# Seven half-size products for three of four second feed-forward products, and strips' low parts on GpSimd in the first attention

## The reference, cut to what matters

```python
h = h + jnp.concatenate([att, ssd], axis=-1) @ w_out[i]
hn = rmsnorm(h, norm_mlp_w[i])
h = h + jnp.square(jax.nn.relu(hn @ w_ff1[i])) @ w_ff2[i]
```

## Time and profile before

| | us |
|---|---|
| median of 3 runs | 1649.72 |
| lowest and highest | 1649.25, 1651.26 |
| the profiled execution | 1650.62 |
| its span in the trace | 1648.9 |

### The profile page before, as it was taken

The page is one execution under the profiler, slowest core; times in us unless marked ns, Lnnn a source line. Parts: engine busy times, 40 slices in busy tenths (PEclk is TensorE's granted clock), DMA queues, the critical chain, the costliest instruction groups (busy, mean ns, idle before and its releaser), DMA issues.

```text
span 1648.9 us, 19185 instructions
## 1 busy us (share of the span) xinstructions
PE 1619.0 (98%) x7688; PEld 1334.3 (81%) x7688; DVE 964.1 (58%) x1388; ACT 670.9 (41%) x1011; POOL 171.4 (10%) x244
## 2 busy tenths in 40 slices
PE   7999999999999999999999999999999999999998
PEld 6878777788888888887788877888888888888787
DVE  6745688674343434656844568544567727735757
ACT  5534375543222313414672146442334414414544
POOL 0001135100000000003710146000000000000000
PEclk9999999999999999999999999999999999999999
DMA  5224231122222222231122221322232222222321
GB/s 186 77 79 146 84 128 52 58 96 102 103 85 95 102 102 101 107 130 72 52 77 103 77 77 51 129 101 81 99 115 103 90 90 102 102 103 84 121 102 52
DMA packets 27992, 157.30 MB, mean 95 GB/s; under 512 B 3776, under 2 KB 6272, under 8 KB 10752
## 3 DMA queue, kind: packets, MB, share of 16 engines
q1 hardware_dynamic: 23184, 145.52, 24.5%
q10 hardware_dynamic: 4720, 10.56, 1.8%
HBM read 151.84 MB, written 4.23 MB: 95 GB/s over the span
## 4 chain that ended last, share of the span: by engine, by line
PE 88%; DVE 7%; issue 2%; ACT 2%; POOL 1%; DMA 0%; POOLq 0%; SPq 0%; DVEq 0%; ACTq 0%
PE bank L586 24%; PE bank L588 24%; PE bank L587 24%; PE bank L594 2%; PE bank L596 2%; PE bank L595 2%; PE bank L789 1%; PE bank L774 1%; PE bank L885 1%; DVE w_lo L1625 1%; DVE w_lo L1618 1%; PE bank L758 1%; PE bank L759 1%; PE bank L1061 0%; PE bank L1063 0%
## 5 line engine op out<-in xcount | busy, mean ns | idle before, releaser
L586 PE MATMUL bank<-a_hi,w_hi 128*128 128x512 f32 x1184 | 467.8, 395 | 9.0 <-DVE w_lo L1820 8.4
L588 PE MATMUL bank<-a_hi,w_lo 128*128 128x512 f32 x1184 | 462.2, 390 | 0.0
L587 PE MATMUL bank<-a_lo,w_hi 128*128 128x512 f32 x1184 | 461.8, 390 | 0.0
L1106 ACT ACTIVATE w_hi<-w_raw 128x2048 fp32r<-128x2048 f32 x120 | 228.9, 1908 | 280.1 <-DMA w_raw<-in_strips 276.7
L1618 DVE TENSOR_TENSOR w_lo<-w_raw,w_hi 128x2048 fp32r<-128x2048 f32 x118 | 270.1, 2290 | 16.4 <-ACT w_hi L1106 16.2
L586 PEld LDWEIGHTS bank<-a_hi,w_hi 128*128 128x128 f32 x1184 | 223.4, 189 | 54.1 <-DVE w_lo L1820 8.4
L588 PEld LDWEIGHTS bank<-a_hi,w_lo 128*128 128x128 f32 x1184 | 222.8, 188 | 46.8
L587 PEld LDWEIGHTS bank<-a_lo,w_hi 128*128 128x128 f32 x1184 | 223.2, 189 | 44.6 <-issue 0.2
L586 PE MATMUL bank<-b_hi,w_hi 128*128 128x512 f32 x560 | 218.2, 390 | 1.1 <-DVE w_lo L1618 0.6
L587 PE MATMUL bank<-b_lo,w_hi 128*128 128x512 f32 x560 | 217.9, 389 | 0.0
L588 PE MATMUL bank<-b_hi,w_lo 128*128 128x512 f32 x560 | 217.8, 389 | 0.0
(11 more groups left out here) (329 smaller groups left out, 2111.7 us busy)
## 6 DMA issues: line engine op xcount, KB each, us to landing
w_raw<-in_strips SPq DMA_DIRECT2D x132, 1024.0 KB, 4.8
...
```

Source lines behind the costliest of these rows:

```text
L586: mm(ps[:, :], w_hi[slot][:, k, cols], hi[:, k, :], start=(k == 0), stop=False)
L587: mm(ps[:, :], w_hi[slot][:, k, cols], lo[:, k, :], start=False, stop=False)
L588: return mm(ps[:, :], w_lo[slot][:, k, cols], hi[:, k, :], start=False, stop=(k == kt - 1))
L1106: run(w_hi[j], w_raw[j], ACT.Copy).then_inc(hi_split, 1)
```

## The change

**Seven products.** For groups 0 to 2 (`SEVEN`), the product of the hidden values (512 tokens x 1024) with 1024 x 1024 of `w_ff2` is no longer made as eight units. Hidden values T are cut into halves by tokens and by features, the weights A into halves by rows and by columns, and Strassen's seven products of sums of such halves give the four quarters of the result. A product is 256 tokens x 512 by 512 x 512: two token tiles, four feature tiles, three matmuls each, so 24 matmuls of 128x512, now with the hidden values as the stationary side. `T_PARTS` and `A_PARTS` say which halves go into product i, and with what sign; five of the seven have a sum on each side.

ACT squares `relu` once, into `hid` (no split). POOL makes the sums: `a_sums` adds two loaded quarters of the weights (`a_part`, 128x2048) into the strip's `w_raw`, `t_sums` adds two halves of `hid` (128x1024) into `t_raw`. ACT makes the high parts (`a_high`, `t_high`), DVE the low parts (`a_low` 128x2048, `t_low` 128x1024). Products 2 and 6 stay in banks 4 to 7 over the three groups; the banks of the other five are added to `added` tiles by DVE (`add_product`). SP loads the quarters instead of `w_ff2` strips (four of 1 MB a group, as many as before), and the first strip of the next `ff1` goes to a tile `spare`.

**The last group** keeps its two phases as they were. During `ff1_3`, DVE makes the quarters of the result out of `added` and the kept banks in eleven operations one behind the other (`c_step`; five of 128x1024, six of 128x512), PE transposes them back to features in eight times four transposes between its matmuls (`turn_c`), and DVE adds these to `x`.

**The first attention.** The low parts of four strips (the last three of `wo_ssd` and the first of `wo_att`), 16 quarters of 128x512, go from DVE to POOL (`low_quarter`), one in every second slot, behind POOL's `normalize` and copies of that slot. A fifth strip stays with DVE.

```diff
+SEVEN = [f"ff2_{g}" for g in range(FF_GROUPS - 1)]
+T_PARTS = [((0, 0), None, 0), ((1, 0), (0, 0), -1), ((0, 0), (1, 1), 1), ((1, 0), (1, 1), 1), ((0, 0), (0, 1), 1), ((1, 1), None, 0),
+           ((0, 1), (1, 1), -1)]
+A_PARTS = [((0, 1), (1, 1), -1), ((0, 0), (0, 1), 1), ((0, 0), (1, 1), 1), ((0, 0), None, 0), ((1, 1), None, 0), ((1, 0), (0, 0), -1),
+           ((1, 0), (1, 1), 1)]
+T_SUMS = [i for i in range(7) if T_PARTS[i][2]]
+A_SUMS = [i for i in range(7) if A_PARTS[i][2]]
+KEPT = {2: 4, 6: 6}
+ADDED = [i for i in range(7) if i not in KEPT]
+A_PLACE = {(0, 1): 0, (1, 0): 0, (1, 1): 1, (0, 0): 2}
+PHASES += [(f"{w}{g}", 7 if f"{w}{g}" in SEVEN else 4) for g in range(FF_GROUPS) for w in ("ff1_", "ff2_")]
...
                                  d["strips"][0][:, h * (SW // 4):(h + 1) * (SW // 4)]).then_inc(x_loaded[h], 16)
                 sp_eng.dma_start(x[:, two, :], d["x_t"][:, two, :]).then_inc(x_loaded[h], 16)
+            def load_part(part, g):
...
+                    if g == 0:
+                        sp_eng.wait_ge(unit_done, 2 * FIRST["ff1_0"])
...
+                    sp_eng.wait_ge(a_sum, A_SUM0 + len(A_SUMS) * g + 2)
+                    load_part((1, 0), g)
...
+                    s = FIRST["wo_ssd"] + 1 + q // 4
+                    j, part = s % W_SLOTS, slice(2 * (q % 4), 2 * (q % 4) + 2)
+                    if q % 4 == 0:
+                        pool.wait_ge(hi_split, s)
+                        pool.wait_ge(strip_split, s)
+                    ins = pool.tensor_tensor(w_lo[j][:, part], w_raw[j][:, part], w_hi[j][:, part].bitcast(F32), ALU.subtract)
+                    if q % 4 == 3:
+                        ins.then_inc(strip_split, 1)
...
+                    if not causal and n < TILES and n % 2 == 0:
+                        low_quarter(n // 2)
...
+            def a_sums(g, i):
+                one, two, sign = A_PARTS[i]
+                s = FIRST[SEVEN[g]] + i
+                for part in (one, two):
+                    pool.wait_ge(part_loaded[A_PLACE[part]], part_count(part, g))
+                pool.wait_ge(unit_done, 2 * (s - W_SLOTS) + 2)
+                pool.tensor_tensor(w_raw[s % W_SLOTS].rearrange("p k n -> p (k n)"), a_part[A_PLACE[one]], a_part[A_PLACE[two]],
+                                   ALU.add if sign > 0 else ALU.subtract).then_inc(a_sum, 1)
+            def t_sums(g, i):
+                one, two, sign = T_PARTS[i]
+                q = 7 * g + i
+                pool.wait_ge(hid_done, HID0 + KT * g + (W4 if one[1] + two[1] == 0 else KT))
+                pool.wait_ge(unit_done, product_done(q - 3))
+                pool.tensor_tensor(t_raw[q % 3], hid_half(one), hid_half(two), ALU.add if sign > 0 else ALU.subtract).then_inc(t_sum, 1)
+            for g in range(len(SEVEN)):
+                a_sums(g, 0)
+                t_sums(g, 1)
+                a_sums(g, 1)
+                a_sums(g, 2)
+                t_sums(g, 2)
+                t_sums(g, 3)
+                t_sums(g, 4)
+                a_sums(g, 5)
+                a_sums(g, 6)
+                t_sums(g, 6)
...
-            def ff_group(g, norm):
-                stream("ff1_0", feature_k, A, ready=wait_tiles(NORMS["mlp"]["lo"]), strips=8 * g, fills=16 * g,
-                       after=(lambda j: direct_sums("mlp") if j == 0 else None) if norm else None)
-                stream("ff2_0", feature_k, B, ready=lambda k: pe.wait_ge(inner_lo, KT * g + k + 1), strips=8 * g, fills=16 * g)
...
+                for i in range(7):
+                    s, q = FIRST[phase] + i, 7 * g + i
+                    slot, hi, lo = s % W_SLOTS, t_hi[q % 3], t_lo[q % 3]
+                    pe.wait_ge(strip_split, s + 1)
+                    pe.wait_ge(t_low_done, T_LOW0 + q + 1)
+                    for t in range(2):
+                        tok = slice(t * P, (t + 1) * P)
+                        if i in KEPT:
+                            ps, first, end = bank[KEPT[i] + t], g == 0, g == len(SEVEN) - 1
+                        else:
+                            f = 2 * ADDED.index(i) + t
+                            ps, first, end = bank[f % 4], True, True
+                            bank_free(phase, f)
+                        for k in range(W4):
+                            mm(ps[:, :], hi[:, k, tok], w_hi4[slot][:, k, :], start=(first and k == 0), stop=False)
+                            mm(ps[:, :], hi[:, k, tok], w_lo4[slot][:, k, :], start=False, stop=False)
+                            last = mm(ps[:, :], lo[:, k, tok], w_hi4[slot][:, k, :], start=False, stop=(end and k == W4 - 1))
+                        last.then_inc(unit_done, 1)
...
+                    pe.wait_ge(c_step, C_STEP0 + 11)
+                if m >= 4:
+                    pe.wait_ge(c_added, C_ADDED0 + m - 3)
+                for t in range(TT):
+                    src = c_part[t // 2, m // 4][:, t % 2, m % 4 * P:(m % 4 + 1) * P]
+                    last = tr(bank[4 + m % 4][:, t * P:(t + 1) * P], src, ident)
+                last.then_inc(c_turned, 1)
+            C_TURNS = {(5, 1): 0, (5, 3): 1, (5, 5): 2, (5, 7): 3, (6, 3): 4, (6, 4): 5, (6, 5): 6, (6, 6): 7}
...
+            for g in range(FF_GROUPS):
+                stream(f"ff1_{g}", feature_k, A, ready=wait_tiles(NORMS["mlp"]["lo"]),
+                       after=(lambda j: direct_sums("mlp") if j == 0 else None) if g == 0 else None,
+                       within=within_last if g == FF_GROUPS - 1 else None)
+                if g < len(SEVEN):
+                    seven(g)
+            stream(f"ff2_{FF_GROUPS - 1}", feature_k, B, ready=lambda k: pe.wait_ge(inner_lo, k + 1))
...
+                for step, i in ((a_high, 2), (t_high, 2), (a_high, 3), (t_high, 3), (a_high, 4), (t_high, 4), (t_high, 5), (a_high, 5),
+                                (a_high, 6), (t_high, 6)):
+                    step(g, i)
+                s = FIRST[f"ff1_{g + 1}"]
+                act.wait_ge(spare_loaded, SPARE0 + 16 * (g + 1))
+                act.wait_ge(unit_done, 2 * (s - W_SLOTS) + 2)
+                run(w_hi[s % W_SLOTS], spare, ACT.Copy).then_inc(hi_split, 1)
+                hi(s + 1)
...
-                        lo_part(FIRST[phase] + 1, n - 2)
                     if lead is None and not wide and n < 4:
                         lo_part(FIRST[phase] + 1, n)
                     for part in range(4):
                         for i in slot_splits(n - part, call, wide, 1) if 0 <= n - part < SLOTS else ():
-                            lo_part(FIRST[phase] + i, part)
+                            if causal:
+                                lo_part(FIRST[phase] + i, part)
+                            elif i == 5:
+                                dve.wait_ge(strip_split, FIRST[phase] + i)
+                                lo_part(FIRST[phase] + i, part)
...
+            def a_low(g, i):
+                s = FIRST[SEVEN[g]] + i
+                j = s % W_SLOTS
+                dve.wait_ge(hi_split, s)
+                src = w_raw[j].rearrange("p k n -> p (k n)") if A_PARTS[i][2] else a_part[A_PLACE[A_PARTS[i][0]]]
+                v.tensor_tensor(w_lo[j].rearrange("p k n -> p (k n)"), src, w_hi[j].bitcast(F32).rearrange("p k n -> p (k n)"),
+                                ALU.subtract).then_inc(strip_split, 1)
...
+                q = 7 * g + i
+                dve.wait_ge(t_high_done, T_HIGH0 + q + 1)
+                src = t_raw[q % 3] if T_PARTS[i][2] else hid_half(T_PARTS[i][0])
+                v.tensor_tensor(t_lo[q % 3], src, t_hi[q % 3].bitcast(F32), ALU.subtract).then_inc(t_low_done, 1)
...
+            def add_product(g, i):
+                for t in range(2):
+                    f = 2 * ADDED.index(i) + t
+                    dst, src = added[i][:, t, :], bank[f % 4][:, :]
+                    dve.wait_ge(unit_done, 2 * (FIRST[SEVEN[g]] + i) + t + 1)
+                    if g:
+                        dve.wait_ge(dve_evac, EVAC0[SEVEN[g - 1]] + f + 1)
+                    ins = v.tensor_tensor(dst, dst, src, ALU.add) if g else v.tensor_copy(dst, src)
+                    ins.then_inc(dve_evac, 1)
...
-                    dve.wait_ge(inner_hi, n + 1)
+                    relu_evac(g, j)
+                    if j == 0 and g:
+                        lo(FIRST[f"ff1_{g}"] + 2)
+                    if j == 3:
+                        lo(FIRST[f"ff1_{g}"] + 3)
+                    if j == 5:
+                        t_low(g, 0)
+                        a_low(g, 0)
+                    if j == 6:
+                        t_low(g, 1)
+                        a_low(g, 1)
+                for step, i in ((add_product, 0), (a_low, 2), (t_low, 2), (a_low, 3), (t_low, 3), (add_product, 1), (a_low, 4), (t_low, 4),
+                                (t_low, 5), (add_product, 3), (a_low, 5), (a_low, 6), (t_low, 6), (add_product, 4)):
+                    step(g, i)
+                s = FIRST[f"ff1_{g + 1}"]
+                dve.wait_ge(hi_split, s)
```

(33 more changed lines are left out.)

192 lines of the change are left out of this document (156 added, 36 removed).

## The result

The changed kernel takes 1688.64 us (median of 4 runs, 1686.43 to 1690.74), the kernel before 1650.05 (4 runs, 1649.25 to 1651.26): ratio 1.0233, 95% interval 1.0215 to 1.0251. It is slower by 38.6 us; I had forecast 1680, between 1655 and 1700. The spans of the two profiled executions lie 36.9 us apart (1685.8 and 1648.9), and all that follows is counted in them.

The account below looks back on a forecast made before the run. PE's matmuls were taken to bound the kernel. -16.3 (fewer matmuls) + 3.5 (transposes) + 2.5 (last group) + 40.5 (POOL/DVE exclusion) = +30.2 us on 1650.6: 1680.8, median 1680, range 1655 to 1700.

Parts of the forecast that it names:

- -16.3 us for fewer matmuls: Groups 0 to 2: seven products replace eight units, 24 matmuls less a group, 5.44 us three times, -16.3 us.
- Transposes +3.5: Last group: eight times four transposes on PE between its matmuls, 0.44 us each time, +3.5 us.
- first wait +2.5: `ff1_3`: PE waits in unit 5 for DVE's eleventh operation on the result's quarters, +2.5 us, at its cheapest 0.
- POOL's price: POOL's two-input sums: 4.5 us for 2048 columns, 2.35 for 1024, 1.27 for a quarter of 512.
- Mutual exclusion: POOL's sums and DVE's low parts never overlap: whichever starts first blocks the other fully; stalls of +40.5 us in three groups.
- The rival of 1639: Long POOL operations exclude DVE for less than their length, so no product is late: 1639 us, chance 0.15.
- 13.5 us of waits a group: Groups 0 to 2: PE's waits before late products, from group 1 scheduled by hand; +40.5 us for three groups.
- The clock: First feed-forward part: the granted clock was read as 1.00; the forecast has no term for a change of it.
- exclusion at the expected prices: POOL and DVE exclusive, a 2048-column sum taking 3.95 to 5.1 us: forecast 1680, own range 1667 to 1688, chance 0.65.
- The first attention, 0: First attention: moving 16 quarters from DVE to POOL taken as 0, with -4.6 to +10 us.
- No more than now: First attention: PE was to wait no more than in the kernel before, where it waits 4.6 us for POOL's scores.

Follow-up runs that it names:

- short_sums: The changed kernel with each POOL sum made of only an eighth of its columns, so the products are of other matrices: 1643.54 us, ratio 0.996.
- ordered_later_turns: The changed kernel with sums on DVE, DVE's and ACT's steps reordered, last group's transposes a unit later, first attention's low parts on DVE: 1640.88 us, ratio 0.9945.
- filled_waits: The changed kernel with 14 additional PE matmuls, results overwritten, before products 2 and 5 of each group: 1697.17 us, ratio 1.0284.

## Why the prediction was right, and where its sizes were off

- **-16.3 us for fewer matmuls: right.** Away from the waits and what follows them the pace is the old one, and without waits (`short_sums`, `ordered_later_turns`) the gain is there.
- **Transposes +3.5, first wait +2.5: right.** Measured 3.6 and 2.5. That the wait can bring half speed (`short_sums`) was not in it.
- **POOL's price: right.** 4.61 us at its shortest for my 4.5, 2.40 for 2.35, 1.28 for 1.27. The figure of the Trainium skill, "GPSIMD Engine Reference", Performance versus the Vector engine, 4497 ns, is 2.4% below the trace's shortest, 4607 ns.
- **Mutual exclusion: right**, the step that decided the sign. The rival of 1639 is out; a time near it, 1643.5, appears only where the sums are short (`short_sums`).
- **13.5 us of waits a group: too much**, 11.5, 11.3 and 10.2 were measured, 33.0 instead of 40.5. Product 1 (1.7 for 1.5) and 2 (3.7 for 3.7) came as reckoned. Product 4 was 1.7 late instead of 6.9, product 5 4.3 instead of 1.3: I had sum 5 ahead of `a_low` 4; on the chip `a_low` 4 was 1 us earlier and went first, and `t_low` 4 then got in ahead of sum 6. `filled_waits` is the other outcome, with 7.0 at product 4 for my 6.9. A hand schedule of two engines that take turns is only as good as its closest meeting.
- **The clock: missing.** I read the granted clock as 1.00 in a part where PE never waited, and priced the waits as if it stayed there. It added 11.5 us, and the restarts, which I had left out too, 2.3; with the waits 7.5 fewer that makes 6.3 us. The forecast for a profiled execution, 1680.8, was 6.7 below the 1687.5 of this one; the median lies another 1.1 higher, where I had put it 0.9 lower. The range held in part by luck: the waits were too many and the clock was missing, and the two errors have opposite signs. Of my narrower range for exclusion at the expected prices, 1667 to 1688, the median is 0.6 beyond the upper end, though POOL's prices were near the middle ones.
- **The first attention, 0: right in size.** Counted from the start of the trace, the changed kernel is some 0.5 us later behind it, less than two medians can tell apart. "No more than now" was not quite so: PE waits 5.2 us for the scores instead of 4.6, and the longest wait is 2.9 instead of 1.7.
